# Layer 1's attention: the last query tile's rotation in pieces over later groups, its scratch in token columns no longer read, and output products two per group

## The reference

```python
q, k, v = split_c(h @ w_qkv, q_g, k_g)            # rms_norm of q and k by head
q, k = apply_rope(q, cos, sin), apply_rope(k, cos, sin)
k_all = jnp.concatenate([k, kc], axis=1)          # 768 keys: latent and context
def block(n):                                     # 128 queries
    s = einsum(q_n, k_all) * HEAD_DIM ** -0.5
    e = exp(s - max(s)); p = e / sum(e)
    return einsum(p, v_all)
y = global_latent_attention(q, k_all, v_all) @ w_out
x = x + gate * rms_norm(y, g)                     # then the gated convolution FFN
```

## Time and profile before

| | us |
|---|---|
| median of three runs | 1519.82 (1517.5 to 1522.52) |
| the profiled execution | 1520.7 |
| its span, first to last instruction | 1518.9 |

### The profile page before, as it was taken

How to read it: one execution, slowest core, us unless ns; L and a number is a source line. 1 busy time by engine, 2 the same in 40 slices (tenths; PEclk the granted TensorE clock), 3 DMA queues, 4 the chain that set the end, 5 groups by cost and what they waited for, 6 DMA issues and landing times.

```text
span 1518.9 us, 21721 instructions
## 1 busy us (share of the span) xinstructions
PE 1437.6 (95%) x7514; PEld 1175.1 (77%) x7514; DVE 1033.1 (68%) x1645; ACT 716.8 (47%) x1245; POOL 570.5 (38%) x509
## 2 busy tenths in 40 slices
PE   4989899999999999999999799899999999999998
PEld 1877567778888888887787588677778888888886
DVE  2468777567678667758879778788876444445445
ACT  3333666444332333224555645588875544443222
POOL 2331545343232232321135422475543444444443
PEclk9999999999999999999999899999999999999999
DMA  8230850222465346333997222010002333333331
GB/s 353 63 99 1 295 178 29 84 98 85 132 186 152 96 140 193 110 111 122 259 244 169 78 73 72 14 57 1 1 25 74 89 106 96 96 97 111 97 97 70
DMA packets 138257, 169.16 MB, mean 111 GB/s; under 512 B 8308, under 2 KB 96632, under 8 KB 137152
## 3 DMA queue, kind: packets, MB, share of 16 engines
q1 hardware_dynamic: 132928, 159.44, 33.1%
q0 software_dynamic: 4608, 8.39, 3.3%
q10 hardware_dynamic: 640, 0.26, 0.1%
HBM read 165.94 MB, written 2.14 MB: 111 GB/s over the span
## 4 chain that ended last, share of the span: by engine, by line
PE 76%; DVE 8%; DMA 5%; issue 5%; ACT 4%; POOL 3%; SPq 0%; POOLq 0%; ACTq 0%; DVEq 0%
PE ps L568 21%; PE ps L569 20%; PE ps L570 20%; PE ps L1728 4%; PE ps L1540 3%; PE ps L1741 2%; PE ps L1743 2%; DMA start_w<-in_ada_w_dram 2%; DMA fast_more<-in_ffn_w_down_dram 2%; PE ps L1637 1%; POOL raw L2569 1%; PE ps L1062 1%; DMA raw<-in_ffn_w_down_dram 1%; POOL ssum L2742 1%; ACT prob L1573 1%
## 5 line engine op out<-in xcount | busy, mean ns | idle before, releaser
L560 POOL TENSOR_TENSOR w_lo<-raw,w_hi 128x1024 fp32r<-128x1024 f32 (+1 forms) x116 | 276.0, 2380 | 473.5 <-ACT w_hi L554 473.5
L568 PE MATMUL ps<-hT_hi,w_hi 128*128 128x512 f32 (+1 forms) x1096 | 387.4, 353 | 4.4 <-DVE hT_lo L2156 3.7
L569 PE MATMUL ps<-hT_lo,w_hi 128*128 128x512 f32 (+1 forms) x1096 | 384.8, 351 | 0.0
L570 PE MATMUL ps<-hT_hi,w_lo 128*128 128x512 f32 (+1 forms) x1096 | 382.5, 349 | 0.0
L568 PEld LDWEIGHTS ps<-hT_hi,w_hi 128*128 128x128 f32 x1096 | 207.2, 189 | 41.3 <-DVE hT_lo L2156 5.6
L570 PEld LDWEIGHTS ps<-hT_hi,w_lo 128*128 128x128 f32 x1096 | 206.4, 188 | 28.9
L569 PEld LDWEIGHTS ps<-hT_lo,w_hi 128*128 128x128 f32 x1096 | 207.1, 189 | 26.8
L554 ACT ACTIVATE w_hi<-raw 128x1024 fp32r<-128x1024 f32 (+1 forms) x137 | 142.3, 1041 | 97.2 <-PE ps L570 78.0
L1602 POOL TENSOR_SCALAR prob<-prob,small 128x768 f32<-128x768 f32 (+3 forms) x108 | 86.0, 797 | 118.7 <-DVE small L1593 118.7
L568 PE MATMUL ps<-w_hi,hT_hi 128*128 128x512 f32 (+1 forms) x288 | 111.3, 387 | 6.6 <-DVE hT_lo L903 2.9
L2459 DVE SCALAR_TENSOR_TENSOR conv_b<-ps,convw,conv_b 128x511 f32<-128x511 f32 (+1 forms) x63 | 39.7, 658 | 114.4 <-ACT conv_b L2402 114.4
(11 more groups left out here) (306 smaller groups left out, 2851.3 us busy)
## 6 DMA issues: line engine op xcount, KB each, us to landing
raw<-in_ffn_w_up_dram SPq DMA_DIRECT2D x84, 512.0 KB, 3.9
ada_w_up<-in_ada_w_dram SPq DMA_DIRECT2D x48, 512.0 KB, 4.1
ada_w<-in_ada_w_dram SPq DMA_DIRECT2D x32, 512.0 KB, 4.8
raw<-in_ffn_w_down_dram SPq DMA_DIRECT2D x56, 256.0 KB, 4.1
raw<-in_ffn_w_down_dram SPq DMA_DIRECT2D x21, 512.0 KB, 3.5
fast_more<-in_ffn_w_down_dram SPq DMA_DIRECT2D x38, 256.0 KB, 3.8
start_w<-in_ada_w_dram SPq DMA_DIRECT2D x8, 1024.0 KB, 8.4
raw<-in_ffn_w_down_dram POOLq DMA_DIRECT2D x24, 256.0 KB, 5.9
```

Of the source, the lines that this page charges most:

```text
L560: by.tensor_tensor(split_to(w_lo, phase, m, width), split_from(phase, m, width), split_to(w_hi, phase, m, width).bitcast(F32), ALU.subtrac ...
L568: nc.tensor.matmul(outp, s_hi, m_hi, start=first, stop=False, skip_group_check=True)
L569: nc.tensor.matmul(outp, s_hi, m_lo, start=False, stop=False, skip_group_check=True)
L570: return nc.tensor.matmul(outp, s_lo, m_hi, start=False, stop=last, skip_group_check=True)
```

## The change

- The last tile (13) is not rotated in `proj_vector`; DVE leaves the projection after group 0's reciprocals, and `attn_vector` no longer waits for the rotation in layer 1. The rotation is a new fill step Q, `last_rope`, in seven pieces at the slots 5, 6, 7, 12, 13, 15 and 16. Its scratch lies in the columns of query tile 3 in `gap[0]`, `hT_hi` and `hT_lo`, which no product reads any more. POOL's root for it (`head_root`) runs at piece 0.
- R of tile 12 stands at the slots 0 and 3, of tile 13 at 22 and 23; tile 13's first waits for Y of tile 0.
- H stands at the slots 5, 6, 7 and 8; the fourth waits for piece 0.
- The products stand two in an iteration: at 9, 10, 12, 13, 15, 16, 18, 19 for tile 0, at 24, 25, 27, 28, 30, 31, 33, 34 for tile 1, at 37, 38, 40, 41, 43, 44, 46, 47 for tile 2; Y at 21, 36 and 49. Each pair waits for the split output of its own group.
- `qk_ss`, `qk_ms` and `qk_r` move to another place; the load of the gate row waits for piece 2 only.

```diff
+LAST_ROPE_AT = (5, 6, 7, 12, 13, 15, 16)
+LAST_TILE_TURNED = 22
+FIRST_HALF_AT = (9, 24, 37)
...
-    at = {3 * u + 5: [("H", u, 0)] for u in range(4)}
-    for first, n in ((0, LAST_TURNS[0]), (6, LAST_TURNS[1])):
-        for b in range(2):
-            at.setdefault(first + 2 * b, []).append(("R", n, b))
-    for n in range(OUT_DONE[1]):
-        first = 3 * (C_KV * n + 5) + 2
+    at = {u + 5: [("H", u, 0)] for u in range(4)}
+    for first, n in ((0, LAST_TURNS[0]), (LAST_TILE_TURNED, LAST_TURNS[1])):
+        at.setdefault(first, []).append(("R", n, 0))
+        at.setdefault(first + (3 if n == LAST_TURNS[0] else 1), []).append(("R", n, 1))
+    for piece, slot in enumerate(LAST_ROPE_AT):
+        at.setdefault(slot, []).append(("Q", piece, 0))
+    for n, first in enumerate(FIRST_HALF_AT):
         for k in range(KC):
-            at.setdefault(first + k, []).append(("W", n, (k,)))
-        at.setdefault(first + KC + 1, []).append(("Y", n, 0))
+            at.setdefault(first + 3 * (k // 2) + k % 2, []).append(("W", n, (k,)))
+        at.setdefault(first + 3 * KC // 2, []).append(("Y", n, 0))
...
+            if l and u == 3:
+                act.wait_ge(s("qk_steps1"), rope_plan(1)[0][LAST_TURNS[1]] + 1)
...
             pe.wait_ge(s("qk_steps1"), base[n + 1])
+            if n == LAST_TURNS[1]:
+                pe.wait_ge(s("mixpost1_ysq"), 1)
...
+                if l and n == LAST_TURNS[1]:
+                    denominator(dve, 1, 0)
...
+                    denominator(dve, 1, 3)
+                    return
...
+        def last_rope(dve, piece):
+
+            n = LAST_TURNS[1]
...
+            if piece == 0:
+                dve.wait_ge(s("qk_sq"), n + 1)
+                nc.vector.reduce_sum(qk_ss[:, 0:heads], sq[:, 0:W].rearrange("p (h d) -> p h d", d=HD),
+                                     AX_X).then_inc(steps, 1)
+            elif piece == 1 or piece == 2:
+                nc.vector.tensor_tensor((a, b)[piece - 1], src,
+                                        qk_tab[:, piece - 1, t, :].unsqueeze(1).broadcast_to([P, heads, HD]),
+                                        ALU.mult).then_inc(steps, 1)
+            elif piece == 3:
...
+                nc.vector.tensor_tensor(a[:, :, 0:half], a[:, :, 0:half], b[:, :, half:HD],
+                                        ALU.subtract).then_inc(steps, 1)
+                nc.vector.tensor_tensor(a[:, :, half:HD], a[:, :, half:HD], b[:, :, 0:half],
+                                        ALU.add).then_inc(steps, 1)
+            elif piece == 4:
...
+                nc.vector.tensor_tensor(a, a, qk_r[:, 0:heads].unsqueeze(2).broadcast_to([P, heads, HD]),
+                                        ALU.mult).then_inc(steps, 1)
+            elif piece == 5:
...
+                nc.vector.tensor_copy(hi, a).then_inc(steps, 1)
+            else:
...
+                nc.vector.tensor_tensor(lo, a, hi.bitcast(F32), ALU.subtract).then_inc(steps, 1)
...
-                            if k == (4 if l == 0 else 0):
-                                pe.wait_ge(s(f"o_split{l}"), 2 * per_tile * (g + 1))
+                            if l == 0 and k == 4:
+                                pe.wait_ge(s("o_split0"), 2 * per_tile * (g + 1))
+                            if l and k % 2 == 0:
+                                pe.wait_ge(s("o_split1"), 2 * (per_tile * g + k // 2 + 1))
...
-            dve.wait_ge(s(f"qk_steps{l}"), rope_plan(l)[0][-1])
+            if l == 0:
+                dve.wait_ge(s("qk_steps0"), rope_plan(0)[0][-1])
...
+                    elif kind == "Q":
+                        last_rope(dve, g)
...
+                    if kind == "Q" and g == 0:
+                        head_root(pool, LAST_TURNS[1])
```

More of the change, by code:

```diff
@@ L334, in hybrid_backbone_kernel @@
         small1, b = sb("small1", [P, 5, 64], F32, b)
+        qk_ss, b = sb("qk_ss", [P, 8], F32, b)
+        qk_ms, b = sb("qk_ms", [P, 8], F32, b)
+        qk_r, b = sb("qk_r", [P, 8], F32, b)
         assert b <= region
@@ L1006, in qks_at, with last_qks @@
             return (qks, qks_b)[n % 2]
+        def last_qks(i):
+            return hT_lo[:, i, (LAT_T - 1) * P:LAT_T * P]
         def tile_batches(l, gi, nt):
@@ L1138, in last_turn @@
             pe.wait_ge(s("qk_steps1"), base[n + 1])
+            if n == LAST_TURNS[1]:
+                pe.wait_ge(s("mixpost1_ysq"), 1)
             if b:
                 pe.wait_ge(s("turned_read1"), tb[n] + b)
+            src = last_qks if n == LAST_TURNS[1] else lambda i: qks_at(1, n)[:, i * P:(i + 1) * P]
             for i in range(4):
                 mm = nc.tensor.transpose(last_turn_bank(n)[:, i * P:(i + 1) * P],
-                                         qks_at(1, n)[:, (4 * b + i) * P:(4 * b + i + 1) * P].bitcast(F32), ident[:, :])
+                                         src(4 * b + i).bitcast(F32), ident[:, :])
             mm.then_inc(s("qk_turned1"), 1)
@@ L1302, in window_sums, with head_root @@
                     reach += max(1, 2 ** step)
+        def head_root(pool, n):
+            heads = token_tiles(1)[n][3]
+            pool.wait_ge(s("qk_steps1"), rope_plan(1)[0][n] + 1)
+            nc.gpsimd.tensor_scalar(qk_ms[:, 0:heads], qk_ss[:, 0:heads], 1.0 / HD, EPS, ALU.mult,
+                                    ALU.add).then_inc(s("qk_rms"), 1)
+            pool.wait_ge(s("qk_rms"), 2 * n + 1)
+            nc.gpsimd.tensor_tensor(qk_r[:, 0:heads], qk_ms[:, 0:heads], minus_half[:, 0:heads],
+                                    ALU.pow).then_inc(s("qk_rms"), 1)
         def proj_pool(pool, l, before):
@@ L1318, in proj_pool @@
                     for t in range(nt):
[L1319 to L1327, removed]
+                        if n < LAST_TURNS[1]:
+                            head_root(pool, n)
                         n += 1
-            if l == 0:
+            if l:
+                for h in FIRST_HEADS:
+                    normalise(pool, 1, h)
+            else:
                 window_sums(pool, (2, 3))
@@ L1358, in v_lo @@
                                             v_hl[:, t, :, 0, :].bitcast(F32), ALU.subtract).then_inc(steps, 1)
+                if l and n == LAST_TURNS[1]:
+                    denominator(dve, 1, 0)
+                    denominator(dve, 1, 1)
+                    score_max(dve, 1, 2)
+                    score_max(dve, 1, 3)
+                    denominator(dve, 1, 2)
+                    denominator(dve, 1, 3)
+                    return
                 if l:
                     nt = PROJ[l][gi][3]
[L1362 to L1368, removed]
                     dve.wait_ge(s("qk_sq"), n + 1)
@@ L1440, in proj_vector @@
                 pool_lo(dve, 0)
+        def last_rope(dve, piece):
+            n = LAST_TURNS[1]
+            base, tb = rope_plan(1)
+            _, kind, t, heads, _ = token_tiles(1)[n]
+            steps, at, W, half = s("qk_steps1"), base[n], heads * HD, HD // 2
+            src = acc_at(1, n, W).rearrange("p (h d) -> p h d", d=HD)
+            cc = slice(t * P, t * P + HD), slice(t * P + HD, (t + 1) * P)
+            a, b = (gap[0][:, :, c] for c in cc)
+            hi, lo = (hT_lo[:, :, c] for c in cc)
+            if piece == 0:
[7 more added lines that the diff above has]
+            elif piece == 3:
+                dve.wait_ge(steps, at + 3)
+                nc.vector.tensor_tensor(a[:, :, 0:half], a[:, :, 0:half], b[:, :, half:HD],
[3 more added lines that the diff above has]
+            elif piece == 4:
+                dve.wait_ge(s("qk_rms"), 2 * n + 2)
+                dve.wait_ge(steps, at + 5)
+                nc.vector.tensor_tensor(a, a, qk_r[:, 0:heads].unsqueeze(2).broadcast_to([P, heads, HD]),
+                                        ALU.mult).then_inc(steps, 1)
+            elif piece == 5:
+                dve.wait_ge(steps, at + 6)
+                nc.vector.tensor_copy(hi, a).then_inc(steps, 1)
+            else:
+                dve.wait_ge(steps, at + 7)
+                nc.vector.tensor_tensor(lo, a, hi.bitcast(F32), ALU.subtract).then_inc(steps, 1)
         def pool_difference(dve, f):
@@ L1707, in attn_tensor @@
                             if k == 0 and g == 0 and l:
+                                pe.wait_ge(s("qk_steps1"), rope_plan(1)[0][LAST_TURNS[1]] + 3)
+                            if k == 0 and g == 1 and l:
                                 pe.wait_ge(s("turned_read1"), rope_plan(1)[1][-1])
-                            if k == (4 if l == 0 else 0):
-                                pe.wait_ge(s(f"o_split{l}"), 2 * per_tile * (g + 1))
+                            if l == 0 and k == 4:
+                                pe.wait_ge(s("o_split0"), 2 * per_tile * (g + 1))
+                            if l and k % 2 == 0:
+                                pe.wait_ge(s("o_split1"), 2 * (per_tile * g + k // 2 + 1))
                             mm = out_half0(pe, l, g, k, first_half_acc(l, g))
@@ L1869, in attn_pool @@
             for kind, g, i in steps:
```

(6 more changed lines are left out.)

11 lines of the change are left out of this document (4 added, 7 removed).

## The result

The changed kernel takes 1523.72 us in the median (1520.31 to 1528.81), the kernel before, run beside it, 1520.59 (1517.5 to 1523.53); the ratio is 1.0023, with a 95% interval of 1.0016 to 1.0030. By the ratio it is slower by about 3.5 us: clear of no change by the interval, and less than the 0.3% (4.6 us) within which the prediction put its forecast of 1522.7 (+2.85).

A forecast was written before the change was run, and what follows sets the result against it. PE, busy for nearly the whole span, was taken as the bound. Start less pile -0.45, products +2.05 and tail +1.25 gave +2.85, so the median 1519.8 becomes 1522.7 us; 8-in-10 range 1518 to 1526.

The forecast's parts named there:

- The start: Start of layer 1's attention: group 1's scores and ACT's work come earlier, PE's 3.23 us idle shrinks; gain 4.7 us.
- E0: ACT's step for group 1 at the attention's start: forecast to begin at 967.9 against 971.51, 3.6 us earlier.
- the clock's share: Part of the gain at the attention's start from the granted clock staying up: 1.1 us, between 0 and 1.7.
- The pile: Iteration 2: three H and the root queue on POOL, delaying T0 of iteration 3; cost 2.35 us.
- Two products behind S1: T0 of iteration 3 to 16: S1's wait for E3 is uncovered, six iterations take 10.53; loss 2.05 us.
- The pieces cost nothing: Pieces 3 to 6 of tile 13's rotation on DVE: no cost, with 0.4 us cover before T2.
- The tail: Iteration 16: Y of tile 2 ahead of the first high part delays the last group; loss 1.25 us.
- S1's wait did not hide: Rival: S1's wait for E3 hides after all, seven iterations fall to 10.0; -3.7, time 1519.0; chance 0.15.
- The clock's fall in the pile: Rival: clock falls in iteration 3 around PE's waits; price 1.7 to 2.5, time 1524.9; chance 0.17.
- The port: Rival: POOL blocks three of DVE's rotation pieces, each held by a probability; +2.3, time 1525.0; chance 0.06.
- step 3: Both products behind S1 in six iterations, T0 of iteration 3 to 16: 134.4 against 132.35, loss 2.05 us.

The follow-up runs named there:

- e1: The changed kernel with the four H back in slots 5, 8, 11 and 14; ratio 1.0021 to the kernel before.
- e2: The changed kernel with the products of tiles 0 and 1 one slot later, one behind S1 and one in the end slot; ratio 1.0003 to the kernel before.
- e7: The kernel before, rotation and H as they were, with the changed kernel's places for products and Y; ratio 1.0029 to the kernel before.
- e8: Changed kernel, products of tiles 0/1 one slot later, tile 2's Y at 50, H at 5, 6, 8, 11, pieces 3-6 at 15, 16, 18, 19; ratio 0.9977.
- e3: The changed kernel with Y of tile 2 in slot 50, the end slot of iteration 16, not 49; ratio 1.0018 to the kernel before.
- e5: The kernel before with only tile 13's rotation changed, its R in slots 27 and 28; H, products and Y as before; ratio 1.0033.
- the three edits: Changed kernel with H back at 5, 8, 11, 14, products of tiles 0/1 one slot later, tile 2's Y at 50; together ratio 0.9988.
- e6: The changed kernel with pieces 3 to 6 of tile 13's rotation in slots 8 to 11; one run, attention length 172.76 us against 172.20.

## Why the prediction was right, point by point

- **The start** was forecast at -4.7 and measured at -5.08 (end of E3 of iteration 1 at 978.68 - 3.01 = 975.67, not 976.05). The order was right to 0.1 (E0 at 967.80, forecast 967.9). Mis-sized was the clock's share: no clock was lost, and I had taken 1.1 of at most 1.7.
- **The pile** was right in mechanism and nearly in its sum: from that E3 to T0 of iteration 3 15.92, forecast 16.05, with waits of 1.02 and 0.93 (forecast 1.05 and 1.3). What it costs against no pile was too small, 2.35 against 2.97 in e1.
- **Two products behind S1** was right in mechanism (e2, e7) and too small by 1.0: 135.38 from T0 of iteration 3 to 16, +3.03, forecast 134.4 and +2.05. The six iterations take 10.60 to 10.65 instead of 10.53, 0.60 together, since S1 behind its idle time takes 0.80 until the first product (1013.71 to 1014.51), where I had 0.70. The one into 8 takes 11.40 and not 11.1, for T2 waits 0.34 for DVE's low part; the rest are 0.1 or less each. Into 13 to 15 it is 29.90, forecast 30.0.
- **The pieces cost nothing** was right for this kernel by two covers. One I had as a number, the 0.4 until T2 needs the low part; in e2 and e8, where S1 does not wait, each pair costs 0.3 to 0.7, so it hangs on S1's wait. The other I had not seen as such: the piled H. The sentence "at their slots POOL is between two probabilities by my count" was right, but my list of endangered pieces (3, 4 and 6) left out piece 5, the copy, which is held as long as piece 3.
- **The tail** was forecast at +1.25 and measured at +0.90 (1129.98 to 1139.98, or 10.00, against 9.10); e3 gives 0.89 back.
- **The rivals.** S1's wait did not hide. The clock's fall in the pile did not come, but stood one product away (e2: 1.26, the forecast's price 1.7 to 2.5). The port did not strike, but stood one H away (e1: 2.1, forecast 2.3; that the sizes agree is luck, since I had three instructions held by a probability each and not two held by an H).

The sum +2.85 against +2.96 is thus better than its terms, by luck: step 3 was short by 1.0, and the start with the pile was off by 0.5 and the tail by 0.35 the other way. The forecast time, 1522.7 against 1523.72, was also short by 0.8 because its base, the median of three runs, was 1519.82 and not 1520.59.

What stays open: in the runs with the moved rotation the ratio gives 0.1 to 1.1 us more than the length does (e5: 2.4), in e7 with the old rotation 0.1. Layer 1's projection is not the place: from ACT's row above, at 886.62 in the trace of before, to the first transposes all twelve traces take 78.2. Whether something further ahead, such as the new place of `qk_ss`, costs some 0.5 us was not tried.

## What to carry to other kernels

Work that fills an engine's waits covers only the wait that it stands ahead of: two products behind S1 cover POOL's wait and leave the one of S1, so spread the fill over all waits of an iteration. Before a step of DVE is moved, look at what POOL runs at that moment, copies included, and before a pile is taken apart, look at what it keeps apart: the three edits that each looked like a plain gain gave back 0.87, 2.55 and 0.78 singly, 5.75 together, and 8 only once the pieces stood clear of the H. Where waits are bunched, write down what PE does between them, since a product less there lost the clock.

## What the runs showed of the hardware

- An operation of POOL of 2.39 held a DVE subtraction of 128x256 and a DVE copy of 128x512 with one input, 0.42 each alone, for 1.90 and 1.91, to 0.29 behind its own end (e1). The hold goes to the end of the single operation: beside POOL's short ones the same pieces took 0.82 and 1.02, and a product of 128x512, 0.69 alone, took 1.24, to 0.54 behind the end of a probability at 991.18 (e6). It works the other way as well: POOL's probability took 1.27 instead of 0.91 behind a DVE subtraction (e6). So engines wait for each other by more than semaphores, other than the first section has it, and such a wait shows as a longer busy time and not as idle time (the 1.90 in e1).
- The granted clock fell from 1.00 to 0.50 behind idle times of PE of 1.03 and 1.61 with one product between them (e2), and behind waits of 0.34 and 0.78 around single batches of transposes (e5); it stayed at 1.00 behind 1.02 and 0.93 with two products between (the changed kernel), and behind 1.18 and 1.39 with two (e6).
